# The tail of a two-layer mixer: other orders on TensorE, ScalarE and VectorE, low parts written into the weight ring

## What is computed

```python
for l in range(DEPTH):                      # DEPTH = 2
    x = x + 0.5 * swiglu_ffn(rms_norm(x, ffn1_norm[l]), ffn1_w_in[l], ffn1_w_out[l])
    h = rms_norm(x, mix_norm[l])
    uv, c_q, c_kv, k_rope, z, xbc, dt_raw, gates = jnp.split(h @ w_in[l], IN_OFFSETS, axis=-1)
    y_a, y_b, y_c = gmlp_mixer(...), mla_mixer(...), ssd_mixer(...)      # 512 columns each
    g = jax.nn.sigmoid(gates).reshape(bsz, s, N_BRANCH, D_MODEL)
    merged = (g[:, :, 0] * (y_a @ w_branch[l, 0])
              + g[:, :, 1] * (y_b @ w_branch[l, 1])
              + g[:, :, 2] * (y_c @ w_branch[l, 2]))
    x = x + merged @ w_out[l]
    x = x + 0.5 * swiglu_ffn(rms_norm(x, ffn2_norm[l]), ffn2_w_in[l], ffn2_w_out[l])
```

## Time and profile before

| | |
|---|---|
| three runs | 1983.67, 1987.09, 1988.6 us (median 1987.09) |
| profiled execution | 1975.48 us, span 1973.8 us |
| TensorE busy | 1875.1 us (95%), 10644 products |
| VectorE busy | 934.4 us (47%) |
| ScalarE busy | 709.9 us (36%) |
| transfers | 293.02 MB, mean 148 GB/s |
| tail of layer 0 | about 395 to 514 us of the span |
| tail of layer 1 | about 1090 to 1209 us |

### The profile page before, as it was taken

The page is one execution under the profiler, slowest core; times in us unless marked ns, Lnnn a source line. Parts: engine busy times, 40 slices in busy tenths (PEclk is TensorE's granted clock), DMA queues, the critical chain, the costliest instruction groups (busy, mean ns, idle before and its releaser), DMA issues.

```text
span 1973.8 us, 25367 instructions
## 1 busy us (share of the span) xinstructions
PE 1875.1 (95%) x10644; PEld 1535.2 (78%) x10644; DVE 934.4 (47%) x1166; ACT 709.9 (36%) x813; POOL 77.9 (4%) x145
## 2 busy tenths in 40 slices
PE   7999999997999999999999978999899999889998
PEld 7998575576899789985755667998787975749996
DVE  4544134467555444441335574545667431234453
ACT  5543213143454345441131343554223121214542
POOL 0000000000000000000000002000361100000000
PEclk9999999998999989999999999999998899989999
DMA  6545434343653565454344437736344223326353
GB/s 235 173 140 191 150 119 152 128 134 106 208 171 128 192 212 172 141 192 140 130 132 133 134 117 121 240 120 212 131 150 115 65 78 131 112 85 213 128 180 129
DMA packets 192244, 293.02 MB, mean 148 GB/s; under 512 B 7218, under 2 KB 126804, under 8 KB 192164
## 3 DMA queue, kind: packets, MB, share of 16 engines
q1 hardware_dynamic: 189908, 287.72, 43.4%
q0 software_dynamic: 1936, 4.14, 2.0%
q10 hardware_dynamic: 320, 0.01, 0.0%
HBM read 289.49 MB, written 2.36 MB: 148 GB/s over the span
## 4 chain that ended last, share of the span: by engine, by line
PE 90%; DVE 4%; DMA 2%; ACT 2%; issue 1%; DVEq 0%; SPq 0%; ACTq 0%
PE acc L221 17%; PE acc L223 17%; PE acc L222 17%; PE acc L189 16%; PE acc L253 7%; PE acc L409 2%; PE acc L2374 1%; PE acc L203 1%; PE acc L2682 1%; PE turn L308 1%; DMA ring<-in_ffn_w_out 1%; DMA ring<-in_ffn_w_in 1%; DVE w_lo L381 1%; PE acc L1161 1%; ACT w_hi L377 1%
## 5 line engine op out<-in xcount | busy, mean ns | idle before, releaser
L381 DVE TENSOR_TENSOR w_lo<-ring,w_hi 128x2048 fp32r<-128x2048 f32 x160 | 362.9, 2290 | 273.1 <-ACT w_hi L377 272.6
L221 PE MATMUL acc<-xT_hi,w_hi 128*128 128x256 f32 x1680 | 477.1, 284 | 3.0 <-DVE w_lo L381 3.0
L223 PE MATMUL acc<-xT_hi,w_lo 128*128 128x256 f32 x1680 | 476.2, 283 | 2.4 <-issue 2.4
L222 PE MATMUL acc<-xT_lo,w_hi 128*128 128x256 f32 x1680 | 476.1, 283 | 0.0
L377 ACT ACTIVATE w_hi<-ring 128x2048 fp32r<-128x2048 f32 x160 | 302.1, 1913 | 221.2 <-DMA ring<-in_ffn_w_out 110.3
L221 PEld LDWEIGHTS acc<-xT_hi,w_hi 128*128 128x128 f32 x1680 | 323.3, 192 | 5.9 <-issue 5.8
L222 PEld LDWEIGHTS acc<-xT_lo,w_hi 128*128 128x128 f32 x1680 | 323.2, 192 | 0.1
L223 PEld LDWEIGHTS acc<-xT_hi,w_lo 128*128 128x128 f32 x1680 | 323.2, 192 | 0.0
L189 PE MATMUL acc<-ring,xT 128*128 128x512 f32 (+2 forms) x736 | 303.2, 571 | 0.8 <-DVE xT L2662 0.8
L189 PEld LDWEIGHTS acc<-ring,xT 128*128 128x128 f32 x736 | 140.2, 192 | 153.9 <-issue 141.3
L221 PE MATMUL acc<-w_hi,hT_hi 128*128 128x512 f32 x440 | 173.0, 393 | 4.7 <-DVE w_lo L381 4.7
(11 more groups left out here) (503 smaller groups left out, 1984.2 us busy)
## 6 DMA issues: line engine op xcount, KB each, us to landing
ring<-in_ffn_w_in SPq DMA_DIRECT2D x88, 1024.0 KB, 5.5
ring<-in_w_in SPq DMA_DIRECT2D x48, 1024.0 KB, 5.1
ring<-in_ffn_w_out SPq DMA_DIRECT2D x44, 1024.0 KB, 4.9
ring<-in_w_branch SPq DMA_DIRECT2D x12, 1024.0 KB, 5.0
ring<-in_w_out SPq DMA_DIRECT2D x12, 1024.0 KB, 5.0
ring<-in_w_gate SPq DMA_DIRECT2D x11, 1024.0 KB, 5.2
ring<-in_w_up SPq DMA_DIRECT2D x11, 1024.0 KB, 7.1
ring<-in_w_down SPq DMA_DIRECT2D x11, 1024.0 KB, 4.9
```

The source lines that it names most:

```text
L221: pe.matmul(o, a_hi, wh, start=start, stop=False)
L222: pe.matmul(o, a_hi, wl, start=False, stop=False)
L223: return pe.matmul(o, a_lo, wh, start=False, stop=stop)
L381: vec.tensor_tensor(w_part(w_lo, r), raw_part(c0, r), w_part(w_hi, r).bitcast(F32), ALU.subtract).then_inc(f.lo, 1)
```

## The change

The following moves; all other code is the same.

- `ring_lo` is the ring's own memory under the type float32r. The low part of a chunk is written over the chunk; `part_lo` is gone and `part_hi` is four deep. The high part of a chunk waits only for the chunk's landing. ScalarE's wait ahead of the first high parts is for step 24 of `sd.vec`, before 20.
- Softmax: both rounds of exponentials come ahead of branch 1's input on ScalarE, and gate 5's sigmoid after them; `qs_vec5` is split by tile and put between the first low parts and gate products on VectorE.
- TensorE: the transposes of attention weights come between branch 0 and branch 1, the attention products between the halves of branch 1.
- The last branch runs m0n0, m0n1, m1n0, m1n1 and the output projection tile by tile within each half n, with the merged transposes of tile 0 ahead of m1n1 and those of tile 1 behind the first 12 products of the projection. VectorE multiplies and adds the last branch per tile and half.
- Norms: the norms at the two layer ends are no longer `apart`: tile 0's transposes leave the FFN's last products and stand behind them. The norm behind the output projection uses `add_norm_vec`, so that tile 0 is added and scaled ahead of tile 1.

```diff
+        ring_lo = nc.alloc_sbuf_tensor_at("ring_lo", [P, RING, SLOT], F32R, offset=nc.sbuf_base - 4 * RING * SLOT)
...
         def part_act(act, s, c, e, hi, k=4, n=512):
             wait_chunk(act, c)
-            if e >= 2:
-                wait_products(act, c - 2)
-            act.activation(hi[:, e % 2], slot(c, k, n), ACT.Copy).then_inc(s.hi, 1)
+            act.activation(hi[:, e % RING], slot(c, k, n), ACT.Copy).then_inc(s.hi, 1)
...
-            vec.tensor_tensor(lo[:, e % 2], slot(c, k, n), hi[:, e % 2].bitcast(F32), ALU.subtract).then_inc(s.lo, 1)
+            vec.tensor_tensor(slot_lo(c, k, n), slot(c, k, n), hi[:, e % RING].bitcast(F32), ALU.subtract).then_inc(s.lo, 1)
...
         def add_norm_vec(vec, add, s, gain):
...
+                if s.apart:
+                    turned(2 * m)
+                    turned(2 * m + 1)
+            if not s.apart:
+                for b in range(4):
+                    turned(b)
...
-        norms_in = [Norm(norms, (20 * l, 32 * l, 12 * l), l < DEPTH, apart=l > 0) for l in range(DEPTH + 1)]
+        norms_in = [Norm(norms, (20 * l, 32 * l, 12 * l), l < DEPTH) for l in range(DEPTH + 1)]
...
+            def last_branch_pe(pe):
+                b = BRANCHES[2]
+                pe.wait_ge(tail.vec, 4)
+                for m in range(MT):
+                    for n in range(2):
+                        ins = split_chunk_pe(pe, tail, G_BR + 4 + n, m, C_BR + 4 + n, 6 + n, yT_hi[:, b], yT_lo[:, b], part_hi)
+                        ins.then_inc(tail.pe if m == 0 else products_done, 1)
+                        if m == 1 and n == 0:
+                            merged_pe(pe, 0)
...
+            def last_branch_vec(vec, n, m):
+                b = BRANCHES[2]
+                vec.wait_ge(br.vec, 2 * n + m + 1)
+                wait_acc_read(vec, G_GATE + 2 * b + n, m)
+                if m == 0:
+                    vec.wait_ge(tail.pe, n + 1)
+                else:
+                    wait_products(vec, C_BR + 4 + n)
+                G = G_BR + 4 + n
+                vec.tensor_tensor(br_t[:, n, m, :], acc[bank(G, m)][:, :], gates[:, m, b * D + n * 512:b * D + (n + 1) * 512],
+                                  ALU.mult).then_inc(acc_read[bank(G, m)], 1)
+                wait_acc_read(vec, G, m)
+                dst = xn[:, m, n * 512:(n + 1) * 512]
+                vec.tensor_tensor(dst, dst, br_t[:, n, m, :], ALU.add).then_inc(br.vec, 1)
...
-                branch_pe(pe, 0)
-                branch_pe(pe, 1)
+                branch_pe(pe, 0, 0)
+                branch_pe(pe, 0, 1)
                 qs_pt_pe(pe)
+                branch_pe(pe, 1, 0)
                 qs_pv_pe(pe)
-                branch_pe(pe, 2)
-                merged_pe(pe)
-                pe.wait_ge(tail.vec, 8)
+                branch_pe(pe, 1, 1)
+                last_branch_pe(pe)
                 for n in range(2):
-                    split_group_pe(pe, tail, G_WO + n, C_WO + 2 * n, 8 + 2 * n, xT_hi, xT_rest, part_hi, part_lo, 2,
-                                   for_x=(n == 1))
+                    for m in range(MT):
+                        pe.wait_ge(tail.vec, 6 + 2 * m)
+                        for i in range(2):
+                            if n == 0 and m == 0 and i == 1:
+                                merged_pe(pe, 1)
+                            ins = split_chunk_pe(pe, tail, G_WO + n, m, C_WO + 2 * n + i, 8 + 2 * n + i, xT_hi[:, 4 * i:4 * i + 4],
+                                                 xT_rest[:, 4 * i:4 * i + 4], part_hi, i == 0, i == 1)
+                            if m == 1:
+                                ins.then_inc(products_done, 1)
+                        if n == 1 and m == 0:
+                            ins.then_inc(tile0_done, 1)
...
-                norm_pe(pe, n1, tiles=(1,) if l > 0 else (0, 1))
+                norm_pe(pe, n1)
```

More of the change, by code:

```diff
@@ L223, in three, with split_chunk_pe @@
             return pe.matmul(o, a_lo, wh, start=False, stop=stop)
[L225 to L239, removed]
+        def split_chunk_pe(pe, s, G, m, c, e, a_hi, a_lo, hi, first=True, last=True):
+            pe.wait_ge(s.lo, e + 1)
+            if first:
+                wait_acc_free(pe, G, m)
+            ms = slice(m * P, (m + 1) * P)
+            for k in range(4):
+                ins = three(pe, acc[bank(G, m)][:, :], a_hi[:, k, ms], a_lo[:, k, ms], hi[:, e % RING, k, :],
+                            slot_lo(c, 4, 512)[:, k, :], first and k == 0, last and k == 3)
+            return ins
         def turned_group_pe(pe, G, c, aT, n_tiles, n, K=KD):
@@ L288, in add_norm_vec, with turned @@
         def add_norm_vec(vec, add, s, gain):
+            def turned(b):
+                vec.wait_ge(s.pe, s.p0 + b + 1)
+                vec.tensor_tensor(quarter(xT, b), turn[b][:, :].rearrange("p (k n) -> p k n", k=4),
+                                  gain.unsqueeze(2).broadcast_to([P, KD, P])[:, 4 * (b % 2):4 * (b % 2) + 4, :],
+                                  ALU.mult).then_inc(s.vec, 1)
             for m in range(MT):
@@ new lines, in branch_gate_vec @@
+            def branch_gate_vec(vec, j, n):
+                b = BRANCHES[j]
+                for m in range(MT):
+                    wait_acc_read(vec, G_GATE + 2 * b + n, m)
+                wait_products(vec, C_BR + 2 * j + n)
+                for m in range(MT):
+                    g = bank(G_BR + 2 * j + n, m)
+                    dst = xn[:, m, n * 512:(n + 1) * 512] if j == 0 else br_t[:, n, m, :]
+                    vec.tensor_tensor(dst, acc[g][:, :], gates[:, m, b * D + n * 512:b * D + (n + 1) * 512],
+                                      ALU.mult).then_inc(acc_read[g], 1)
@@ L1363, in merged_pe @@
+            def merged_pe(pe, m):
+                pe.wait_ge(br.vec, 6 + 2 * m)
+                for hf in range(2):
+                    b = 2 * m + hf
                     for k in range(4):
@@ L1366, in merged_pe, with merged_vec @@
                     ins.then_inc(mt.pe, 1)
-            def merged_vec(vec):
-                for b in range(4):
-                    m, hf = b // 2, b % 2
+            def merged_vec(vec, m):
+                for b in range(2 * m, 2 * m + 2):
                     vec.wait_ge(mt.pe, 1 + b)
-                    vec.tensor_copy(xT[:, 4 * hf:4 * hf + 4, m * P:(m + 1) * P], heads(turn[b][:, :], 4)).then_inc(mt.vec, 1)
+                    vec.tensor_copy(quarter(xT, b), heads(turn[b][:, :], 4)).then_inc(mt.vec, 1)
             def tail_part_act(act, *es):
@@ L1574, in pe_program @@
                 norm_pe(pe, n2)
-                ffn_pe(pe, f2, n2, C_FFN2, G_FFN2, lambda e: norm_pe(e, n_next, tiles=(0,)), asides={4: params2_pe, 6: s5_c_pe} if l == DEPTH - 1 else {})
+                ffn_pe(pe, f2, n2, C_FFN2, G_FFN2, lambda e: None, asides={4: params2_pe, 6: s5_c_pe} if l == DEPTH - 1 else {})
             def sync_program(sync):
```

137 lines of the change are left out of this document (63 added, 74 removed).

## The result

The changed kernel took 1965.88 us (median of 4 runs, 1961.67 to 1968.82) against 1986.19 (4 runs), a ratio of 0.9896 with the interval 0.987 to 0.9923. Timed again, 6 runs gave 1964.67 and a ratio of 0.9902 (0.9884 to 0.992). The direction was right.

What follows compares the result with a forecast made beforehand. TensorE, busy 95% of the span, was taken to be bound by idle time and lower clock. -25.5 + 6.8 + 0.6 + 3.4 - 1.0 = -15.7 us, with one clock drop of 1.9 about -14: 1973 us, range 1966 to 1981.

Steps and rivals of the forecast that it cites:

- Where the idle time lay, and that it goes: Mixer's last part: four TensorE waits, 21.8 us over two layers, counted as taken away by the new order.
- The new wait behind the exponentials: Before branch 0's second half, TensorE waits for ScalarE's gate 5 sigmoid: 3.4 us per layer, 6.8 in all.
- The transposes' own wait: Fifth group of attention-weight transposes waits for VectorE's first copy: 0.3 us per layer, 0.6 in all.
- The rival, that the gate's accumulator is free in time: Rival A: no sigmoid wait at branch 0's second half, fifth transposes wait 1.8 us; 1968 us, chance 0.12.
- The drain that the Trainium skill adds: ScalarE's table switches: 1.38 us beside the load, making the sum 2.8 us worse over two layers; left out of the forecast.
- Merged transposes: Tile 0's merged transposes wait for the last branch's third quarter multiplied and added: 1.7 us per layer, 3.4 in all.
- The clock: TensorE's clock behind the tail stalls: 2.4 + 1.3 us regained, less one new drop of 1.9 us.
- Rival B: Clock falls behind every new stall, the gate's and the merged one: four drops, 9.6 us; 1981 us, chance 0.22.
- The ring: Low parts written over the ring's chunks, four high parts: subtraction stays 2.29 us, no cost or gain.
- rival C: Ring subtraction takes 4.4 us, stalls of 3.7, 1.7, 4.5, 2.1, 1.5 beside the gate's; 1994 us, chance 0.04.
- Norms: Norms at the two layer ends: net 0.5 us gained at each, 1.0 in all.
- nobody is helped: 0: Norm behind the output projection: tile 0 is early without benefit, 0 us, with 0.3 either way.

Runs made afterwards that it cites:

- attn_back: Changed kernel with TensorE's transposes of attention weights and attention products back behind both halves of branch 1: 1981.43 us (12 runs).
- gate_early: Changed kernel with gate 5's sigmoid moved on ScalarE ahead of branch 1's input and the high parts of chunks 4 and 5: 1965.93 us (6 runs).
- gate_late: Changed kernel with gate 5's sigmoid put behind chunk 6's high part too, lengthening the known wait: 1977.55 us.
- second pair of profiles: Profiles of a further execution each of the kernel before and the changed kernel, both unchanged; their spans differ by 19.6 us.
- after_again: Changed kernel, unchanged, timed more often: median 1964.67 us (6 runs).
- norms_back: Changed kernel with all norms as before, at both layer ends and behind the output projection: 1967.05 us against 1964.67 in the same session.

## Why the prediction was right and wrong, step by step

- **Where the idle time lay, and that it goes: right.** 21.8 us of waits at four places; three are gone, the fourth is 0.4 per layer. `attn_back` brings two of them back at their old size or above.
- **The new wait behind the exponentials: right to two tenths.** 3.4 forecast; 3.40 and 3.56 measured. `gate_early` and `gate_late` show that it is ScalarE's order. The transposes' own wait was 0.3 forecast, 0.4 measured. The rival, that the gate's accumulator is free in time, is out. The drain that the Trainium skill adds to a table load (ScalarE: Activation LUTs, What ACT_TABLE_LOAD costs) does not show here either: from 437.35 it runs 1.28 us and the sigmoid begins at 438.64.
- **Merged transposes: the term was mis-sized.** The step "They need the third quarter of the last branch multiplied and added" is wrong. They wait for the second sum, both halves of tile 0, and the third quarter's products run meanwhile. 0.4 in place of 1.7 per layer, 2.6 us in two. It was there to be read in the code: `merged_pe(pe, 0)` waits for six steps of `br.vec`, four of branch 1 and two of the last branch. `last_branch_pe` puts the third quarter ahead of the transposes only in TensorE's queue.
- **The clock: the term that failed.** The step "Taken away: 21.8 of idle and 2.4 + 1.3 of clock" with "I take one drop of the mean size, 1.9" amounts to 1.8 us of clock in all. By the mean clocks of the executions it is up to 6.7 us, and by TensorE's busy time in the second pair of profiles 6.1; the first pair has only 2.7. Both halves were read from a single execution that, of 30 of this kernel, had the highest clock. They were also read too small in that execution: the clock was already low from 478 to 483 (0.52), ahead of the twelve products that the prediction counted, so that layer 0 lost some 3.5 us on work and not 2.4 (7.05 us of work lie in the low stretch). And the first profile had drops behind one pair of waits in each layer, while in other executions the wait ahead of the last branch costs clock too, as in 1161 to 1164 above: in two of eight places in the kernels with the old tail, and in both layers of `attn_back`.
- **Rival B**, the clock falling behind every new stall: in the first profile it falls behind the gate's stall in both layers (0.62 and 0.71 in the windows above) and not behind the merged one, which is only 0.4 long. In `after_again` it falls in layer 1 alone. With `norms_back` and `attn_back` it is seven stalls of eight, in one of them already within the wait. Half of the rival came true, but the old stalls turned out to cost more than I had given them, so that the sum moved the other way. The rule of the Trainium skill on waits between bursts (TensorE: Matmul & The Clock Gate, HAM oscillation) fits the gate's stall (seven of eight) and the pair at the projection (eight of eight), and the wait of 3.13 us ahead of the old last branch only in two of eight.
- **The ring: right.** 0 in time, 2285 ns per subtraction, so the condition of rival C did not arise. The sizes of its five stalls and its gain of 6 us at 3.5 us per subtraction were given without their working, and no run tests them.
- **Norms: small in sum, but not as said.** The layer ends gained 1.8 us in the profiles for a forecast of 1.0. Behind the output projection, where "nobody is helped: 0" stood, the new order is followed by a lower clock that costs some 2 us in layer 0. The total is not resolved below 3 us.
- **The size, then.** The forecast of -14 had -11.0 of waits, -1.0 for the norms and -1.8 of clock; the waits came out 2.2 us larger, by the merged transposes, and the clock up to 4.9. Another 0.9 us of the distance between 1973 and 1965.88 lies in the median of before, 1987.09 when forecast and 1986.19 with the fourth run.

The sum with the measured sizes: -21.8 + 7.0 + 0.8 + 0.8 = -13.2 of waits, -6.7 of clock by the mean clocks, together -19.9, against -20.3 in the first timing and -19.5 in the second. That it closes so well is in part luck, since 1970 us per unit of clock is an upper price.

## What to carry to other kernels

Price a stall of TensorE in dense work at more than its length: in this kernel putting 10 us of waits back in four stalls cost 14 to 17, whereas lengthening two stalls that were there already by 10.9 us cost 11 to 13. In these two runs it was the number of separate stalls that cost extra, so it pays more to remove a stall altogether than to shorten one. Read the clock from many executions before putting it in a sum. Compare two kernels between the same instructions, stage by stage, before trusting the difference of two spans. And when one queue's order is freed, walk the other queue to the same place before expecting the gain.

## What the runs showed of the hardware that I had not expected

The mean granted clock of one and the same kernel ranged from 0.967 to 0.975 over 29 executions, while their spans ranged over 12 us, from 1977.6 to 1989.9; a line through them puts two thirds of the variance down to the clock. The level of it belongs to the kernel: means of 0.970 to 0.972 for all four versions that have the waits around attention's products, 0.975 to 0.977 for the five that have neither these nor the longer wait at the gate. And the drop mostly comes late: in the changed kernel a wait of 3.4 us ran wholly at a granted 1.00, and the products behind it at 1.2 GHz for part of the next 3 us. In the waits of 9 us (`gate_late`) it came within the wait.
